# Three phase ends of a fused three-block kernel reordered: last projection and gate of the neighbourhood phase, last mLSTM head, last delta head

## The reference

```python
h = num / jnp.maximum(jnp.abs(den), jnp.exp(-m_t))[..., None]     # each direction
...
h = h_fwd + h_bwd
mu = h.mean(-1, keepdims=True)
var = jnp.mean(jnp.square(h - mu), -1, keepdims=True)
h = ((h - mu) * lax.rsqrt(var + MH_EPS)) ...
return (h * norm_g * jax.nn.sigmoid(o.astype(jnp.float32))).astype(v.dtype)
```

```python
qkv = jax.nn.silu(short_conv(h_qkv, conv_w))
...                                   # gated delta rule in both directions: o2
o = o2[:B].astype(jnp.float32) + o2[B:, ::-1].astype(jnp.float32)
o = rms_norm(o, norm_g) * jax.nn.silu(z)
...
o_na = neighborhood_attention(q_na, k_na, v_na, rpb[l])
o_na = rms_norm(o_na, na_norm_g[l])
mix = jnp.einsum('bte,ed->btd', jnp.concatenate([o_gdn, o_na], axis=-1), w_out[l])
x = layer_norm(DEEPNORM_ALPHA * x + mix, ln1_g[l], ln1_b[l])
```

## Time and profile before

| | |
|---|---|
| median of three runs | 4099.3 us |
| the three runs | 4102.55, 4099.3, 4094.27 us |
| the profiled execution | 4100.63 us |
| its span, first to last instruction | 4098.9 us |
| mean granted TensorE clock | 0.967 |
| instructions | 52918 |

### The profile page before, as it was taken

One profiled execution on the slowest core, in us unless ns is written; L12 is line 12 of the kernel. 1 busy time (PEld: TensorE's weight loads), 2 busy tenths in 40 slices (PEclk: granted clock), 3 DMA queues, 4 the chain that ended last, 5 costly groups with the idle time before them and its releaser, 6 DMA issues. The chain is left out here.

```text
span 4098.9 us, 52918 instructions
## 1 busy us (share of the span) xinstructions
PE 3858.4 (94%) x21004; PEld 3042.9 (74%) x21004; DVE 1734.6 (42%) x2847; ACT 1305.1 (32%) x2309; POOL 466.5 (11%) x334
## 2 busy tenths in 40 slices
PE   9998999989997889999999999999788889999998
PEld 5787887867666668888888766767577668888886
DVE  3343422224566643222222355666566543323234
ACT  4355222223565342111111164555333232111112
POOL 1000000020004040000000131112423130000001
PEclk9999999999999999999999999999898999999999
DMA  2011011121113111111111112111200101111111
GB/s 90 26 31 57 26 47 52 46 82 37 34 32 93 36 47 47 46 46 48 49 46 50 37 38 70 54 51 52 89 32 33 37 32 51 46 51 46 51 46 57
DMA packets 87422, 199.42 MB, mean 49 GB/s; under 512 B 18872, under 2 KB 20344, under 8 KB 87240
## 3 DMA queue, kind: packets, MB, share of 16 engines
q1 hardware_dynamic: 87240, 196.96, 15.2%
HBM read 183.75 MB, written 15.14 MB: 49 GB/s over the span
## 5 line engine op out<-in xcount | busy, mean ns | idle before, releaser
L407 ACT ACTIVATE b_ffn_wh<-b_ffn_raw 128x1024 fp32r<-128x1024 f32 (+1 forms) x136 | 141.9, 1043 | 612.9 <-PE b_ffn_space L387 612.9
L386 PE MATMUL b_ffn_space<-b2f_x_lo,b_ffn_wh 128*128 128x512 f32 x800 | 316.0, 395 | 0.0
L385 PE MATMUL b_ffn_space<-b2f_x_hi,b_ffn_wh 128*128 128x512 f32 x800 | 314.1, 393 | 0.0
L387 PE MATMUL b_ffn_space<-b2f_x_hi,b_ffn_wl 128*128 128x512 f32 x800 | 311.9, 390 | 0.0
L464 DVE TENSOR_TENSOR b_ffn_wl<-b_ffn_raw,b_ffn_wh 128x1024 fp32r<-128x1024 f32 (+2 forms) x140 | 179.2, 1280 | 214.9 <-ACT b_ffn_wh L407 183.9
L385 PE MATMUL b_ffn_space<-b3f_hidden_hi,b_ffn_wh 128*128 128x512 f32 x512 | 199.2, 389 | 0.0
L386 PE MATMUL b_ffn_space<-b3f_hidden_lo,b_ffn_wh 128*128 128x512 f32 x512 | 199.2, 389 | 0.0
L387 PE MATMUL b_ffn_space<-b3f_hidden_hi,b_ffn_wl 128*128 128x512 f32 x512 | 199.2, 389 | 0.0
L386 PE MATMUL b_ffn_space<-b3f_x_lo,b_ffn_wh 128*128 128x512 f32 x480 | 189.3, 394 | 0.0
L385 PE MATMUL b_ffn_space<-b3f_x_hi,b_ffn_wh 128*128 128x512 f32 x480 | 187.3, 390 | 0.5 <-DVE b_ffn_wl L464 0.5
L387 PE MATMUL b_ffn_space<-b3f_x_hi,b_ffn_wl 128*128 128x512 f32 x480 | 186.9, 389 | 0.0
(11 more groups left out here) (628 smaller groups left out, 9098.4 us busy)
## 6 DMA issues: line engine op xcount, KB each, us to landing
b_ffn_raw<-w SPq DMA_DIRECT2D x62, 512.0 KB, 3.5
b_ffn_raw<-w_ffn SPq DMA_DIRECT2D x44, 512.0 KB, 3.6
all_x<-xT SPq DMA_DIRECT2D x16, 512.0 KB, 6.5
b_ffn_raw<-w_ffo SPq DMA_DIRECT2D x16, 512.0 KB, 3.5
g_heads<-na_done SPq DMA_DIRECT2D x16, 512.0 KB, 2.6
b_out_raw<-w_out SPq DMA_DIRECT2D x12, 512.0 KB, 3.6
na_feed_raw<-w_gqkv SPq DMA_DIRECT2D x24, 256.0 KB, 2.7
b_head_raw<-w_bv SPq DMA_DIRECT2D x16, 256.0 KB, 3.3
```

The source lines that it names most:

```text
L385: nc.tensor.matmul(acc[i][:, c], wh[i][:, wk], xh[:, c], start=(k == 0), stop=False)
L386: nc.tensor.matmul(acc[i][:, c], wh[i][:, wk], xl[:, c], start=False, stop=False)
L387: last = nc.tensor.matmul(acc[i][:, c], wl[i][:, wk], xh[:, c], start=False, stop=(k == st.KT - 1))
L407: nc.scalar.activation(wh[i][:, 0:st.KT * P], raw[i][:, 0:st.KT * P], ACT.Copy).then_inc(hi_done, 1)
```

## The change

It has four parts.

- The input is rejoined during the last projection. `Feed` gets a semaphore `passed`, raised by the first matmul of each k but the first in the last block; the join of block k waits for the matmul of k + 1, and only the last join of a half waits for the whole product. The due times follow PE's. `pair_time` goes from 13.0 to 5.2 behind a pair's last unit, for all four pairs, and the last norm's root from 4.0 to 2.9 behind its start.
- The last gate block is taken straight from PSUM by ACT's Silu; it has no Tanh, and no work on POOL. SP stores it in two halves, each as soon as it is taken.
- The last mLSTM head is finished in pairs of chunks, from the middle outwards (3 and 4, then 2 and 5, 1 and 6, 0 and 7), each pair through denominators, sums and statistics. The normalisation signals after each half, PE transposes half 0 after the first signal, the root and the transposes get earlier due times, and a mix waits for the gate of its own half only, in all heads.
- The last delta head is squared and reduced by the same pairs, and scaled in two halves, each transposed when it is ready.

```diff
@@ Feed.products
-                    self.nc.tensor.matmul(acc[:], wh[:, wk], xh[:, c], start=(k == 0), stop=False)
+                    first = self.nc.tensor.matmul(acc[:], wh[:, wk], xh[:, c], start=(k == 0), stop=False)
+                    if self.passed is not None and b + 1 == len(self.plan) and k:
+                        first.then_inc(self.passed, 1)
@@ mlstm, PE
-                            yield (h + 1) * HEAD + 29.5 + 2.0 * half
+                            yield (h + 1) * HEAD + (29.5 if h + 1 < M_H else 14.5) + 2.0 * half
...
+                                if h + 1 == M_H:
+                                    pe.wait_ge(normed, h + 2)
@@ mlstm, ACT
-                        yield (h + 1) * HEAD + 24.5
+                        yield (h + 1) * HEAD + (24.5 if h + 1 < M_H else 12.5)
@@ mlstm, DVE
+                def outwards(h, body, hsum):
+                    at = (h + 1) * HEAD
+                    for i in range(DT // 2):
+                        yield at + (i - 0.8) * STEP
+                        pair, both = slice(3 - i, 5 + i, 2 * i + 1), (3 - i, 4 + i)
+                        for dr in range(2):
+                            ve.wait_ge(num_ready[dr], DT * h + DT // 2 + 1 + i)
+                        last_col = num[:, h % 2, :, pair, M_DH]
+                        nc.vector.scalar_tensor_tensor(out=den[:, :, pair], in0=last_col, scalar=-1.0, in1=last_col, op0=ALU.mult, op1=ALU.max)
+                        ve.drain()
+                        for dr in range(2):
+                            nc.vector.tensor_tensor(den[:, dr, pair], den[:, dr, pair], gate_cols[:, 3, pair, 32 * dr + h], ALU.max)
+                        ve.drain()
+                        nc.vector.reciprocal(den[:, :, pair], den[:, :, pair]).then_inc(den_ready, 1)
+                        ve.wait_ge(den_ready, h + i + 1)
+                        for t in both:
+                            nc.vector.tensor_scalar(hsum[:, t, :], hsum[:, t, :], den[:, 0, t:t + 1], None, ALU.mult).then_inc(divided, 1)
+                        ve.wait_ge(divided, DT * h + 2 * i + 2)
+                        for t in both:
+                            last = nc.vector.scalar_tensor_tensor(out=hsum[:, t, :], in0=body[:, 1, t, :], scalar=den[:, 1, t:t + 1], in1=hsum[:, t, :],
+                                                                  op0=ALU.mult, op1=ALU.add)
+                        last.then_inc(added, 1)
+                        ve.wait_ge(added, h + i + 1)
+                        for t in both:
+                            nc.vector.bn_stats(stats[:, t, :], hsum[:, t, :])
+                        ve.drain()
+                        for t in both:
+                            last = nc.vector.bn_aggr(mv[:, t, :], stats[:, t, :])
+                    last.then_inc(mv_ready, 1)
+                    yield at + 12.7
...
+                    for half in range(2):
+                        yield at + 12.8 + half
+                        for t in range(4 * half, 4 * half + 4):
+                            last = nc.vector.tensor_scalar(hsum[:, t, :], hsum[:, t, :], mv[:, t, 0:1], rstd[:, t:t + 1], ALU.subtract, ALU.mult)
+                        last.then_inc(normed, 1)
...
-                            if half == 0:
-                                for i in range(2):
-                                    ve.wait_ge(feed.taken[i], h + 1)
+                            ve.wait_ge(feed.taken[half], h + 1)
@@ delta_rule, POOL (last head)
+                        for i in range(NG):
+                            yield finish_time(h) - 3.0 * (NG - 1 - i)
+                            for dr in range(2):
+                                pool.wait_ge(sum_done[dr], DT * h + NG + 1 + i)
+                            nc.gpsimd.tensor_tensor(osq[:, outward(i)], osum[:, outward(i)], osum[:, outward(i)], ALU.mult).then_inc(squared, 1)
+                        for half in range(2):
...
+                            nc.gpsimd.tensor_tensor(osum[:, t, :], osum[:, t, :], ss[:, t, None].broadcast_to([P, NG, P]), ALU.mult).then_inc(normed, 1)
@@ delta_rule, DVE (last head)
+                            for i in range(NG):
+                                yield finish_time(h) + 1.2 - 3.0 * (NG - 1 - i)
+                                ve.wait_ge(squared, h + i + 1)
+                                ve.wait_ge(normed, h)
+                                last = nc.vector.tensor_reduce(ss[:, outward(i)], osq[:, outward(i)], AX_X, ALU.add)
+                            last.then_inc(ss_ready, 1)
@@ HeadNorms.roots
-            yield self.starts[m] + 4.0
+            yield self.starts[m] + (4.0 if m + 1 < len(self.jobs) else 2.9)
@@ neighbourhood_attention
+                if m + 1 == len(heads):
+                    return nc.scalar.activation(done[m % 3][:, c], acc[:], ACT.Silu)
...
-            return begin + DT * (b + 1) * SPACE + 13.0
+            return begin + DT * (b + 1) * SPACE + 5.2
...
+                            for half in range(2):
+                                yield curve_time(m, half) + 0.5
+                                c = slice(half * HALF, (half + 1) * HALF)
+                                sp.wait_ge(feed.taken[half], i + 1)
+                                sp.dma_start(dram["g_heads"][m * P:(m + 1) * P, c], done[m % 3][:, c]).then_inc(stored[m % 3], 16)
...
-                for m in range(len(heads)):
+                for m in range(len(heads) - 1):
...
-                            yield plan[-1][0] + plan[-1][1] * (half + 1) / 2 + 0.5 + 0.7 * k
-                            if k == 0:
+                            yield plan[-1][0] + plan[-1][1] * (half * DT + k + 1) / (2 * DT) + 0.4
+                            if k + 1 < DT:
+                                ve.wait_ge(feed.passed, (DT - 1) * half + k + 1)
+                            else:
                                 ve.wait_ge(feed.acc_ready[half], len(kinds))
...
-                    for m, i in enumerate(heads):
+                    for m, i in enumerate(heads[:-1]):
```

More of the change, by code:

```diff
@@ L602, with __init__ @@
     PIECE = DT // 2 * P
-    def __init__(self, ph, name, pair, weights, takes, plan, slots=2, lead=8.0):
+    def __init__(self, ph, name, pair, weights, takes, plan, slots=2, lead=8.0, passing=False):
         self.nc, self.pair, self.weights, self.takes, self.plan, self.slots, self.lead = ph.nc, pair, weights, takes, plan, slots, lead
@@ L2416, in states @@
                                                                in1=kv[:, 0:W], op0=ALU.mult, op1=ALU.add).then_inc(state_done[dr], 1)
+                def outwards(h, body, hsum):
[28 more added lines that the diff above has]
+                    yield at + 12.7
+                    ve.wait_ge(std_ready, h + 1)
+                    nc.vector.reciprocal(rstd[:], rstd[:])
+                    ve.drain()
+                    for half in range(2):
[3 more added lines that the diff above has]
+                        last.then_inc(normed, 1)
@@ L2422, in finishing @@
                         hsum = body[:, 0]
-                        yield at + 2.2 * STEP
-                        for dr in range(2):
-                            ve.wait_ge(num_ready[dr], DT * (h + 1))
-                        last_col = num[:, h % 2, :, :, M_DH]
-                        nc.vector.scalar_tensor_tensor(out=den[:], in0=last_col, scalar=-1.0, in1=last_col, op0=ALU.mult, op1=ALU.max)
-                        ve.drain()
-                        for dr in range(2):
-                            nc.vector.tensor_tensor(den[:, dr, :], den[:, dr, :], gate_cols[:, 3, :, 32 * dr + h], ALU.max)
@@ L2431, in finishing @@
-                        ve.drain()
-                        nc.vector.reciprocal(den[:], den[:]).then_inc(den_ready, 1)
-                        for t in range(DT):
-                            if t % 2 == 0:
-                                yield at + 9.0 + 0.6 * t
-                            if t == 0:
-                                ve.wait_ge(den_ready, h + 1)
-                            nc.vector.tensor_scalar(hsum[:, t, :], hsum[:, t, :], den[:, 0, t:t + 1], None, ALU.mult).then_inc(divided, 1)
@@ L2439, in finishing @@
-                        for t in range(DT):
-                            if t % 2 == 0:
-                                yield at + 14.0 + 0.7 * t
-                            ve.wait_ge(divided, DT * h + t + 1)
-                            last = nc.vector.scalar_tensor_tensor(out=hsum[:, t, :], in0=body[:, 1, t, :], scalar=den[:, 1, t:t + 1], in1=hsum[:, t, :],
-                                                                  op0=ALU.mult, op1=ALU.add)
-                        last.then_inc(added, 1)
@@ L2446, in finishing @@
-                        for t in range(0, DT, 2):
-                            yield at + 19.7 + 0.6 * t
-                            if t == 0:
-                                ve.wait_ge(added, h + 1)
-                            for i in range(t, t + 2):
```

(20 more changed lines are left out.)

92 lines of the change are left out of this document (74 added, 18 removed).

## The result

The changed kernel takes 4107.2 us (median of 16 runs, 4100.2 to 4116.9), the kernel before, run beside it, 4099.2 (16 runs, 4091.6 to 4109.3). The ratio is 1.0023, 95% interval 1.0014 to 1.0031: slower, by 8 us from median to median (the interval's ends are +5.7 and +12.7), where 4094 was predicted with a range to 4100 and 0.05 for slower. The profiled execution took a span of 4104.5.

A forecast was written before the change was run, and what follows sets the result against it. PE, busy 94% of the span, bounds the kernel, and at three ends chains on other engines while PE runs dry. +2.8 - 6.1 - 2.1 = -5.4 from 4100.6 gives 4095.2; the median, 1.3 lower, 4094; 8 in 10 within 4087 to 4100.

The forecast's parts named there:

- I cost this at nothing: Middle of neighbourhood phase: moving the other three pairs' norms and three head norms 7.8 forward costs nothing; bounds -4 and +2.
- Rival (d): Neighbourhood phase: the three moved sums stall PE, via a square delayed on ACT, with half clock after; +23, 4117; chance 0.05.
- Rival (b): Neighbourhood phase: the moved norms relieve PE, four of 4.8 us of waits for na_near go; 4090; chance 0.14.
- mLSTM, +2.8: End of mLSTM: pairs bring the statistics 3.9 later, transposing after four of eight normalisations saves 1.05; net +2.8, bounds +0.8 and +4.3.
- the one generator: End of mLSTM: `finishing` yields the pairs after head 2's mix, so all four run in a row, none woven into the recurrence.
- Rival (c): End of mLSTM: the pairs do overlap the recurrence, three of four, 8.1 us, leave the chain; 4086; chance 0.08.
- Neighbourhood end, -6.1: End of neighbourhood phase: earlier square, sums, root and joins, spreads at full clock; net -6.1, bounds -7 and -3.5.
- rival (a): End of neighbourhood phase: the clock has fallen by the spreads, 1.85 less is won; 4096; chance 0.15.
- After the pause of 3.9 and not after the one of 2.4: End of neighbourhood phase, kernel before: where PE's clock fell, near 2916.2; with pauses of 1.8 and 0.8, full clock was taken.
- Rival (e): End of neighbourhood phase: the last store holds the end, landing in 8.7; -2.0 instead of -6.1, 4098; chance 0.08.
- Delta, -2.1: End of delta rule: 2.7 saved at the end, two recurrence steps about 0.3 longer each; net -2.1, bounds -3.2 and -1.0.
- hidden today by the same chain: End of neighbourhood phase: POOL's multiplications for the last gate block, which the change removes, were said to cost no time before.

## Why the prediction was wrong

- **The step that failed** is "I cost this at nothing", of the norms of the other three pairs and the head norms behind them, with bounds of -4 and +2. The forecast's own range left out the +2 as well as the -4: with it, the terms' bounds add up to 4101 and not 4099. Measured: +10.0 in the phase, +8 in the median when done alone. The argument weighed only the square on ACT against the sum on PE, "about 2 behind" in the plan. The sum did wait, for 0.8 us in all; but each norm also has two spreads on PE, and the second waited for the scaling of the first half on DVE, for 4.9 us in all. With the pauses came half clock, 5.3 us. The plan moved more than I named, too: by the due times six of the eight head norms change their start and not three, and pair 1's norm overtakes one of them (its square on ACT stands at 2712.3, ahead of a head's at 2726.7, where it stood behind one before: 2706.2, then 2722.7). I looked at one of the norm's seven handovers, in a phase where PE's queue is in order and has no slack.
- **Rival (d)** had the sign, the victim (PE) and the half clock behind a pause, but another place (the square on ACT), and 0.05 was far too little. Its size of 4.5 us a norm and more was never met: over three norms it is 3.3, of pauses of 0.8 to 2.1 us and of half clock.
- **Rival (b)**, that the moved norms relieve PE, had a small part of the truth: of the 4.8 us of waits for na_near 3.1 went, but those for na_wide grew by 2.1. The 1.0 that is left stands against 5.7 of new waits for norms.
- **mLSTM, +2.8:** right. The pairs cost 3.6 (forecast 3.9), the half-wise turn brings 1.0 (1.05), net +2.6; the pairs stood behind the one generator as argued. The reasoning that instructions in small dependent groups cost more than their fixed term held too: twelve more instructions, 3.6 us. The Trainium skill, "VectorE: DVE Perf Modes", section "The TRN2 errata — SBUF-src ops pay a fixed extra latency per instruction", would have 1.9 for them, an estimate from its 150 cycles; the trace has the larger number.
- **Rival (c)** failed by the one generator, as argued. The run with the pairs woven in adds a reason that I had not named: the phase got 1.3 us shorter and not 8.1, as far as its scatter lets one tell, since DVE has little room there.
- **Neighbourhood end, -6.1:** -4.9. Everything arrived in the forecast order and within 0.3 us; 1.3 is missing because both spreads ran below full clock, rival (a) in the larger part. How much the low clock takes is partly luck: behind the same pause of 1.78 the first spread took 1.31, 1.53, 1.55 and 1.77 in the four kernels with this end. "After the pause of 3.9 and not after the one of 2.4" was no rule: here it fell within the spread behind a pause of 1.78.
- **Rival (e)** is out: the last store was issued at 2924.7, the two half stores took 2.0 to land, and the last scaling starts at 2929.68.
- **Delta, -2.1:** -2.3 in the two traces, made of -2.8 at the end and +0.3 for each of two steps, each as forecast. The end's listed terms add up to 5.4 and not to the 5.7 that I took; it measured 5.6.
- **The sum:** +2.6 + 10.0 - 4.9 - 2.3 = +5.4 by the traces, just below the measured +5.7 to +12.7. What the last 2 or 3 us of the median are stays open. The stretch ahead of the mLSTM phase, with the same instructions in every kernel, alone lies between 1232.5 and 1241.3 us from trace to trace.

## What to carry to other kernels

When an edit of one due time serves the last item of a loop, give it to the last item only, or follow every instruction of every other item through all its queues, and count the handovers in which an in-order engine without slack is the one that waits. A pause of 2 us on such an engine can cost more than itself, since the work behind it may run at half clock: of the 10 us here 5.3 were that. Splitting a chain into groups that cannot overlap with anything costs 1.0 to 1.6 us a group here; signalling half of an existing loop (the half-wise turn) brought 1.0 in the trace.

## What the runs showed of the hardware

The 16 joins that I read as one block of equal instructions are not equal. First DVE's joins in the kernel before (shortest, median, longest in ns) and POOL's two multiplications beside the last of them, then the first of these two in the kernel with the delta part alone:

```profile
L3909 DVE TENSOR_TENSOR all_x<-b3v_x_hi,b3v_x_lo x16: 676/680/1777, 2901.4 to 2914.8; 128x512 f32<-128x512 f32 x16
```

```profile
2909.59 1.85 POOL L3805 TENSOR_TENSOR na_gate<-na_gate,na_done 128x512 f32<-128x512 f32 x1 [3.43 <-ACT na_gate L3954]
2911.52 1.59 POOL L3807 TENSOR_TENSOR na_done<-na_done,na_gate 128x512 f32<-128x512 f32 x1
```

```profile
2910.10 4.86 POOL L3829 TENSOR_TENSOR na_gate<-na_gate,na_done 128x512 f32<-128x512 f32 x1 [3.43 <-ACT na_gate L3978]
```

In the kernel before a join takes 0.68 us alone, and the four that took 1.75 to 1.78 each ran beside one of POOL's four multiplications of the last gate block; in the second kernel the same multiplication took 4.86 instead of 1.85, while the joins beside it kept 0.68, and the block of 16 took 11.90 us instead of 14.04. One of the two stands still for the other, and which one changed between two executions of the same two instruction streams; of the eight traces with these streams, seven are like the first and one like the second. It is worth 2.1 us at this end (14.6 instead of 17.7 in all, with a spread at full clock). The Trainium skill, "SBUF — State Buffer", section "Who interferes with whom", has this: a DVE instruction with two SBUF inputs and a GpSimd instruction that reads SBUF contend for a shared read port, which one of them holds alone. The trace agrees, and shows a stream of joins holding it from instruction to instruction. The prediction called POOL's multiplications "hidden today by the same chain"; in the kernel before the second pair of them lengthened that chain by these 2.1 us.
